# Two PSUM banks in place of four for the two attention output projections of a three-layer transformer kernel

## The reference, cut to what matters

```python
# layer 2: differential attention, 8 heads of 2 x 64, values of 128 columns
p = softmax(where(causal, q @ k^T * scale, NEG_INF))   # two maps for each head
a = p[:, :, 0] - lam * p[:, :, 1]
o = rms_norm_2(a @ v, subln) * (1 - lambda_init)
x = x + o.reshape(B, S, 1024) @ w_o                     # stage "do" of the kernel
x = x + swiglu(rms_norm_2(x, ffn_norm[0]), ...)         # stages "f2..."
# layer 3: sliding window attention with sinks, 16 query heads on 4 key heads
o = softmax_with_sink(q @ kw^T) @ vw
x = x + o.reshape(B, S, 1024) @ w_o                     # stage "so"
x = x + swiglu(rms_norm_2(x, ffn_norm[1]), ...)         # stages "f3..."
```

## Time and profile before

| | us |
|---|---|
| time, median of 3 runs | 1927.33 |
| lowest and highest run | 1927.11, 1927.91 |
| time of the profiled execution | 1927.91 |
| its span | 1926.0 |
| TensorE busy with matmuls | 1885.4 (98%) |
| VectorE busy | 1172.1 (61%) |
| ScalarE busy | 769.3 (40%) |
| GpSimd busy | 269.3 (14%) |

### The profile page before, as it was taken

How to read it: one execution, slowest core, us unless ns; L and a number is a source line. 1 busy time by engine, 2 the same in 40 slices (tenths; PEclk the granted TensorE clock), 3 DMA queues, 4 the chain that set the end, 5 groups by cost and what they waited for, 6 DMA issues and landing times.

```text
span 1926.0 us, 24010 instructions
## 1 busy us (share of the span) xinstructions
PE 1885.4 (98%) x9191; PEld 1518.9 (79%) x9198; DVE 1172.1 (61%) x1929; ACT 769.3 (40%) x1644; POOL 269.3 (14%) x212
## 2 busy tenths in 40 slices
PE   6999998999999999999999999999999999999999
PEld 5887777888888888766678888888877788888887
DVE  8467899655354457488775535445978675445453
ACT  4445666333232233366643323223356543223231
POOL 3000342111011011011121101101210021011010
PEclk9999999999999999999999999999999999999999
DMA  6232000223333233322222333333341133323333
GB/s 218 62 99 66 23 1 1 81 94 99 99 95 94 96 90 104 103 70 78 61 88 88 99 99 97 92 97 90 97 109 50 49 99 96 92 97 99 99 93 93
DMA packets 51249, 166.53 MB, mean 86 GB/s; under 512 B 6848, under 2 KB 7232, under 8 KB 50880
## 3 DMA queue, kind: packets, MB, share of 16 engines
q1 hardware_dynamic: 51136, 165.00, 28.1%
HBM read 155.01 MB, written 2.10 MB: 82 GB/s over the span
## 4 chain that ended last, share of the span: by engine, by line
PE 85%; DVE 10%; ACT 2%; issue 2%; DMA 1%; SPq 1%; POOL 0%; DVEq 0%; ACTq 0%
PE bank L899 24%; PE bank L901 24%; PE bank L900 24%; PE bank L1009 2%; PE bank L873 1%; PE bank L874 1%; PE bank L875 1%; PE bank L1065 1%; PE bank L922 1%; DVE WL L1473 1%; PE bank L1109 1%; PE bank L1098 1%; PE bank L1089 1%; DVE HX L1850 1%; DVE SM L1688 1%
## 5 line engine op out<-in xcount | busy, mean ns | idle before, releaser
L1193 ACT ACTIVATE WH<-RAW 128x512 fp32r<-128x512 f32 (+2 forms) x584 | 331.6, 614 | 765.3 <-PE bank L901 681.6
L1473 DVE TENSOR_TENSOR WL<-RAW,WH 128x512 fp32r<-128x512 f32 (+2 forms) x584 | 450.5, 806 | 73.7 <-ACT WH L1193 67.5
L899 PE MATMUL bank<-HH,WH 128*128 128x512 f32 x1056 | 425.0, 402 | 14.8 <-DVE WL L1473 9.7
L899 PE MATMUL bank<-GH,WH 128*128 128x512 f32 x1088 | 435.0, 400 | 0.0
L901 PE MATMUL bank<-GH,WL 128*128 128x512 f32 x1088 | 424.3, 390 | 0.0
L900 PE MATMUL bank<-GL,WH 128*128 128x512 f32 x1088 | 423.8, 389 | 0.0
L901 PE MATMUL bank<-HH,WL 128*128 128x512 f32 x1056 | 412.5, 391 | 0.0
L900 PE MATMUL bank<-HL,WH 128*128 128x512 f32 x1056 | 412.2, 390 | 0.0
L899 PEld LDWEIGHTS bank<-HH,WH 128*128 128x128 f32 x1056 | 198.9, 188 | 61.3 <-DVE WL L1473 10.3
L899 PEld LDWEIGHTS bank<-GH,WH 128*128 128x128 f32 x1088 | 204.7, 188 | 44.3 <-issue 3.0
L900 PEld LDWEIGHTS bank<-GL,WH 128*128 128x128 f32 x1088 | 204.8, 188 | 43.2 <-issue 3.1
(11 more groups left out here) (228 smaller groups left out, 1975.8 us busy)
## 6 DMA issues: line engine op xcount, KB each, us to landing
RAW<-in_wgu SPq DMA_DIRECT2D x132, 512.0 KB, 3.5
RAW<-in_wd SPq DMA_DIRECT2D x48, 512.0 KB, 3.5
RAW<-in_wd SPq DMA_DIRECT2D x24, 384.0 KB, 3.1
RAW<-in_da_qk SPq DMA_DIRECT2D x16, 512.0 KB, 3.6
TMP<-TMP SPq DMA_DIRECT2D x104, 64.0 KB, 2.0
RAW<-in_w_inh SPq DMA_DIRECT2D x12, 512.0 KB, 3.5
RAW<-in_w_in SPq DMA_DIRECT2D x8, 512.0 KB, 6.5
RAW<-in_w_out SPq DMA_DIRECT2D x8, 512.0 KB, 3.6
```

Source lines behind the costliest of these rows:

```text
L899: e.matmul(b, w_h, hi[st.x][k], start=(k == 0), stop=False)
L1193: e.activation(whs[s % NW][:, a:b], raw[s % NR][:, a:b], ACT.Copy).then_inc(S["wh"], 1)
L1473: e.tensor_tensor(wls[s % NR][:, a:b], raw[s % NR][:, a:b], whs[s % NW][:, a:b].bitcast(F), ALU.subtract).then_inc(S["wl"], 1)
```

## The change

Stages do and so use banks 0 and 1 in place of banks 0, 1, 4 and 5. The tables follow: do and so lose the waits for the last exponential of the softmax (semaphore ex at 128 and at 160); the first four units of f2g0 and f3g0, which still use banks 0, 1, 4 and 5, wait for residual additions 6 and 7 of the stage before (banks 0 and 1) and for that last exponential (banks 4 and 5), in place of residual additions 4 to 7. The planner is run on the new tables, so the order of the steps on each engine may change also elsewhere. No arithmetic changes.

```diff
-    add("do", 8, 8, "a", "h4", (0, 1, 4, 5))
+    add("do", 8, 8, "a", "h4", (0, 1))
...
-    add("so", 8, 8, "b", "h8", (0, 1, 4, 5))
+    add("so", 8, 8, "b", "h8", (0, 1))
...
-                 "qk": [("e_dvv", 4), ("e_dvv", 5)], "do": [("qn", "qk", 14), ("qn", "qk", 15), ("ex", "d", 31), ("ex", "d", 31)],
-                 "f2g0": [("resv", "do", m) for m in (4, 5, 6, 7)],
+                 "qk": [("e_dvv", 4), ("e_dvv", 5)], "do": [("qn", "qk", 14), ("qn", "qk", 15)],
+                 "f2g0": [("resv", "do", 6), ("resv", "do", 7), ("ex", "d", 31), ("ex", "d", 31)],
...
-                 "sq": [("qn", "ks", 0), ("qn", "ks", 1)], "so": [("qn", "sq", 6), ("qn", "sq", 7), ("ex", "s", 31), ("ex", "s", 31)],
-                 "f3g0": [("resv", "so", m) for m in (4, 5, 6, 7)]}
+                 "sq": [("qn", "ks", 0), ("qn", "ks", 1)], "so": [("qn", "sq", 6), ("qn", "sq", 7)],
+                 "f3g0": [("resv", "so", 6), ("resv", "so", 7), ("ex", "s", 31), ("ex", "s", 31)]}
...
-               ("do", 2): ("ex", 128), ("do", 3): ("ex", 128), ("f2g0", 0): ("do_o", 5), ("f2g0", 1): ("do_o", 6),
-               ("f2g0", 2): ("do_o", 7), ("f2g0", 3): ("do_o", 8),
+               ("f2g0", 0): ("do_o", 7), ("f2g0", 1): ("do_o", 8), ("f2g0", 2): ("ex", 128), ("f2g0", 3): ("ex", 128),
...
-               ("so", 2): ("ex", 160), ("so", 3): ("ex", 160), ("f3g0", 0): ("so_o", 5), ("f3g0", 1): ("so_o", 6),
-               ("f3g0", 2): ("so_o", 7), ("f3g0", 3): ("so_o", 8)}
+               ("f3g0", 0): ("so_o", 7), ("f3g0", 1): ("so_o", 8), ("f3g0", 2): ("ex", 160), ("f3g0", 3): ("ex", 160)}
```

## The result

The change makes the kernel slower: 1943.91 us median (1942.37 to 1944.4, 4 runs) against 1927.62 us (1927.11 to 1927.94, 4 runs). The ratio is 1.0084, 95% interval 1.0066 to 1.0101, or 16.3 us. The forecast was 1940.8 us in a range of 1934.5 to 1944.5. The profiled execution took 1941.7 us, 13.8 us more than that of before. Lines of kernel.py after line 742 stand two lines earlier than before: L897 to L899 are the matmuls of a triple, L907 is lz1, L912 lz4.

A forecast was written before the change was run, and what follows sets the result against it. TensorE, busy 98% of the span, was taken as the bound. +10.5 us at full clock and +3.0 us for the clock made +13.5 us on 1927.91 us, 1941.4, corrected to 1940.8 us for a slow profiled execution; range 1934.5 to 1944.5.

The forecast's parts named there:

- The sum at full clock: Stages do and so together, all terms without any fall of TensorE's clock: +10.5 us.
- 13 and 8 displaced triples: Triples of do and so that move behind the softmax's end for lack of open banks: +8.8 and +5.4 us.
- The last head: End of layer two's softmax, in do: without triples queued ahead, its waits shrink, -2.0 us.
- Handover: In do and so, a unit waits for its bank to be read by a residual addition: +0.3 us in each.
- lz1's wait: End of do: TensorE's 1.55 us stall vanishes because units no longer end in a bunch, -1.5 us.
- The clock: TensorE's clock halves in do's gap, at even chance in so's, and an old fall may vanish: +3.0 us net.
- The fall near 1380 us: The existing drop of TensorE's clock there may vanish as everything shifts: -1.5 us at an even chance.
- A: Rival: the clock holds in both gaps, 1937.8 us, or 1936.3 without the old fall; chance 0.20.
- B: Rival: the clock falls in both gaps and the new order adds a stall elsewhere, 1944 us; chance 0.12.
- the main case: Clock falls in do's gap, with or without so's: 1938.8 to 1943 us, forecast 1940.8; chance 0.60.
- C: Rival: in do the change doesn't bind, VectorE hides the moved triples, only so pays +4.9 us: 1932.2 us; chance 0.05.
- D: Rival: the planner holds back early triples as filler for the softmax's tail, so the kernel gets faster, 1924 us; chance 0.03.

The follow-up runs named there:

- (4): Changed kernel's step order, planned for two banks, but do and so write to four banks with the old waits: 1943.15 us, ratio 1.0083.
- (6): Kernel before with stage do on bank 0 alone, so left on four banks: 1948.94 us, ratio 1.0111.
- (5): Kernel before with stages do and so on three banks (0, 1, 4): 1931.03 us, ratio 1.0019.
- so only: Kernel before with only stage so on banks 0 and 1, do left on four: 1934.95 us, ratio 1.0038.
- the same, second profile: The changed kernel, unaltered, run and profiled again: 1942.47 us, ratio 1.0076.
- do only: Kernel before with only stage do on banks 0 and 1, so left on four: 1935.42 us, ratio 1.0041.
- (7): Kernel before with two planner costs raised, so lz1 after do and lz4 stand later in TensorE's queue: 1926.43 us, ratio 0.9994.
- (9): Kernel before with unit 2 of so on the norms' bank 3 in place of bank 4: 1926.51 us, ratio 0.9999.
- experiment 3: Changed kernel plus 13 throw-away triples on TensorE in the gaps at the end of both softmaxes: 1938.42 us, ratio 1.0058.

## Why the prediction was right, and what in it was too small

**Where the time goes.** Right, and shown from both sides: the order alone makes the loss (4), fewer open units make it larger (6), a third one leaves 3.5 us of it (5), and the changed kernel's gap has idle time in front of just the rows named.

**The sum at full clock.** Forecast +10.5 us, measured with filler +11.0 us (interval 8.3 to 14.1, from its ratio); among runs of equal mean clock it is 10.5 and 10.4 us (one run against four at 1.000, three against four at 0.999). By terms: 13 and 8 displaced triples, since 50 ran after the gap in both stages. The last head gives back 1.75 us (2.0 forecast) and the end of layer three's softmax 0.7 us (6.67 to 5.97 us from weighting to k = 7; 0.8 forecast), but only while the clock holds. Handover 0.26 us (0.3); but in do the kernel before had paid as much already: 982.66 to 983.65 us is 0.99 us between two of its triples, 0.31 above the pitch. So this term was counted once too often for do, which fits the 0.2 us by which do came out lower. lz1's wait of 1.55 us gone (1.5). In stretches: do +5.4 us of 5.6, so +5.2 us of 4.9.

**The clock.** The mechanism was right, this term was mis-sized: "+2.8 us for do" measured 3.9, 2.0 and 1.1 us in three profiles of the same two-bank do (49.82, 47.96 and 46.97 less 45.92); so's "+1.9 us with an even chance" measured 1.1, 2.7 and 3.9 us (45.04, 46.67 and 47.83 less 43.92). The clock fell in so every time; taking half of the term was the mistake, and a second fall in one tail, which came in so in three of four profiles (not in the first of the changed kernel, but in so only, order only and the second), wasn't thought of. By the medians (16.3 or 14.9 less 11.0 us) the clock costs 4 to 5 us in all, against 3.0 forecast.

Two parts of it can be read apart, as differences to the kernel with filler in us: from the last weighting to the first triple with k = 7 (the chain), and from there to lz1 (the triples).

| profile | do, chain | do, triples | so, chain | so, triples |
|---|---|---|---|---|
| changed kernel | 1.7 | 2.2 | 0.0 | 1.1 |
| the same, second profile | 0.0 | 2.0 | 1.5 | 1.2 |
| do only | 0.0 | 1.1 | | |
| so only | | | 2.5 | 1.4 |

For the triples the prediction had 2.2 us less 0.3 in each stage, read at the kernel's start (its division, (14.48 - 9.70) / 2, gives 2.4). For the chain it had 0.9 us in do, for the sum alone and not for the values' product, and nothing in so. So the step that was too small is the tail's own matmuls at the low clock: where the clock falls early enough to meet them, they hold up everything behind.

By the Trainium skill, TensorE: Matmul & The Clock Gate, "HAM oscillation — how this bites in real kernels", work that is interrupted by a long wait goes on at half the clock. These profiles agree with it in both gaps, in do and in so, and the sum with that rule in both was +15.2 us. In so it took no single long wait: none in the gap was longer than 2.08 us, and matmuls ran between them.

**The fall near 1380 us.** It stayed away in the first profile of the changed kernel, which makes up nearly all of the 1.85 us that the middle stretch is shorter. In do only and with three banks it came, at 1385 and 1381 us. So it is chance from run to run, as forecast. By size the price of 1.5 us holds roughly: in the 19 runs of (7) the median of those with a clock below 1.000 is 1.9 us above that of the others. It makes up much of the spread of those runs; in the 20 runs beside (9) the two groups overlap.

**Rivals.** A, the clock holds: only with filler. B, stalls elsewhere: none, the waits near lz4 are the same 0.91 us. But the measured median, 1943.9 us, lies in B's band (1943 to 1946), 0.9 above that of the main case: the clock's cost in the two gaps took the place of the stalls that B needed. C and D: refuted by the time, and by the counts, since 13 and 8 triples did move behind the gap.

## What to carry to other kernels

Where an in-order engine has to bridge a serial tail, count what it may run before the tail's result is in: here open accumulators x 7 blocks. What had run by then with all accumulators, less that count with fewer, is the work that moves behind the tail: 27 - 14 = 13 and 22 - 14 = 8 triples here, 27 - 21 = 6 and 1 with three banks. Work that wouldn't have fitted into the tail anyway isn't lost. Take off what the emptier queue gives back, and add what the clock costs, in the tail's own matmuls and after the gap; throw-away matmuls in the gap measure that share by itself.

## What was not expected

The prediction had no such remedy; it came up with experiment 3, whose expectation then forecast it. Throw-away work made the changed kernel 4 to 5 us faster, 13 more triples on the busiest engine, since they kept its clock at 2.4 GHz. Not expected was that the same program with the same order would lose from 2.0 to 3.9 us in the same gap; in the two profiles it goes with when in the gap the clock fell (978.6 or 973.2 us). Nor was it expected that the clock could fall twice around one gap.
